# The second half of w_o in another order: one context tile between the image tiles, and the norm's first sum one tile later

## The reference: two layers of a hybrid block

```python
def rmsnorm(x, g):
    xf = x.astype(jnp.float32)
    y = xf * lax.rsqrt(jnp.mean(xf * xf, axis=-1, keepdims=True) + EPS)
    return (y * g.astype(jnp.float32)).astype(x.dtype)

def mixer_output(attn, other, pool_w, pool_scale, sconv_w, w_o):
    ...
    return jnp.concatenate([attn, pool_out, conv_out], axis=-1) @ w_o

def conv_ffn(h, w_up, w_conv, w_down):
    g, u = jnp.split(h @ w_up, 2, axis=-1)
    return (jax.nn.silu(dwconv3(g, w_conv)) * u) @ w_down

        # for each of the two layers i
        x = x + g1x * mixer_output(attn_x, rest_x, *out_w)
        x = x + g2x * conv_ffn(rmsnorm(x, norm2_g[i]) * (1 + sc2x) + sh2x, *ffn_w)

        if i < DEPTH - 1:
            attn_c = attend(qn_c, qr_c, kn_c, kr_c, v_c)
            ctx = ctx + g1c * mixer_output(attn_c, rest_c, *out_w)
            ctx = ctx + g2c * conv_ffn(rmsnorm(ctx, norm2_g[i]) * (1 + sc2c) + sh2c, *ffn_w)
```

## Time and profile before

| what | value |
|---|---|
| median of 3 runs | 1477.76 us (1477.02 to 1477.85) |
| profiled execution, its own time | 1477.17 us |
| span of its trace | 1475.4 us |
| TensorE matmuls | 1422.5 us, 96% of the span |
| VectorE | 1015.6 us, 69% |
| ScalarE | 520.1 us, 35% |
| ScalarE's split of a chunk (line 1009) | 180 of them, mean 1054 ns |
| VectorE's split of a chunk (line 1318) | 180 of them, mean 1240 ns |

### The profile page before, as it was taken

How to read it: one execution, slowest core, us unless ns; L and a number is a source line. 1 busy time by engine, 2 the same in 40 slices (tenths; PEclk the granted TensorE clock), 3 DMA queues, 4 the chain that set the end, 5 groups by cost and what they waited for, 6 DMA issues and landing times.

```text
span 1475.4 us, 20621 instructions
## 1 busy us (share of the span) xinstructions
PE 1422.5 (96%) x7932; PEld 1230.0 (83%) x7932; DVE 1015.6 (69%) x1546; ACT 520.1 (35%) x819; POOL 81.8 (6%) x139
## 2 busy tenths in 40 slices
PE   6999799999999999999999998989999999999998
PEld 4789688888888888888888888868998888888887
DVE  5588988669967566656666678788758555655555
ACT  4352765334321121212112224466535332223222
POOL 0024600000000000000000000350000000000000
PEclk9999999999999999999999999999999999999999
DMA  9732011413643343234333311301022332322324
GB/s 386 283 132 86 1 44 44 143 65 107 217 139 100 100 146 124 98 101 142 112 93 122 125 60 58 115 15 44 15 76 97 101 100 93 102 89 85 107 94 140
DMA packets 42984, 158.62 MB, mean 108 GB/s; under 512 B 5169, under 2 KB 6577, under 8 KB 41777
## 3 DMA queue, kind: packets, MB, share of 16 engines
q1 hardware_dynamic: 42928, 157.87, 31.5%
HBM read 155.76 MB, written 2.10 MB: 107 GB/s over the span
## 4 chain that ended last, share of the span: by engine, by line
PE 80%; DVE 13%; ACT 2%; DMA 2%; issue 2%; SPq 0%; DVEq 0%; ACTq 0%
PE ps L675 62%; PE ps L624 4%; PE ps L626 4%; PE ps L625 4%; DVE ada_out L1329 2%; DVE w_lo L1318 1%; DVE tmp L1407 1%; DMA ada_step<-in_w_step 1%; DVE H_lo L1416 1%; PE ps L826 1%; DVE part_sums L1569 1%; DVE ss L1396 1%; PE ps L638 1%; DMA w_raw<-in_w_main 1%; PE ps L845 1%
## 5 line engine op out<-in xcount | busy, mean ns | idle before, releaser
L675 PE MATMUL ps<-H_hi,w_hi 128*128 128x512 f32 (+1 forms) x1280 | 449.5, 351 | 6.4 <-DVE H_lo L1416 3.0
L675 PE MATMUL ps<-H_lo,w_hi 128*128 128x512 f32 (+1 forms) x1280 | 448.1, 350 | 0.0
L675 PE MATMUL ps<-H_hi,w_lo 128*128 128x512 f32 (+1 forms) x1280 | 447.7, 350 | 0.0
L1009 ACT ACTIVATE w_hi<-w_raw 128x1024 fp32r<-128x1024 f32 x180 | 187.5, 1054 | 421.6 <-PE ps L675 366.3
L675 PEld LDWEIGHTS ps<-H_hi,w_hi 128*128 128x128 f32 x1280 | 242.6, 190 | 40.7 <-issue 3.7
L675 PEld LDWEIGHTS ps<-H_hi,w_lo 128*128 128x128 f32 x1280 | 242.6, 190 | 31.7
L675 PEld LDWEIGHTS ps<-H_lo,w_hi 128*128 128x128 f32 x1280 | 242.7, 190 | 31.0
L1429 DVE SCALAR_TENSOR_TENSOR X<-ps,mod,X 128x512 f32<-128x512 f32 (+1 forms) x296 | 180.7, 644 | 113.2 <-PE ps L675 85.2
L1318 DVE TENSOR_TENSOR w_lo<-w_raw,w_hi 128x1024 fp32r<-128x1024 f32 x180 | 221.5, 1240 | 37.7 <-ACT w_hi L1009 36.7
L675 PE MATMUL ps<-inner_hi,w_hi 128*128 128x512 f32 (+1 forms) x528 | 188.1, 356 | 3.4 <-DVE w_lo L1318 1.6
L675 PE MATMUL ps<-inner_lo,w_hi 128*128 128x512 f32 (+1 forms) x528 | 187.2, 355 | 0.0
(11 more groups left out here) (195 smaller groups left out, 1854.0 us busy)
## 6 DMA issues: line engine op xcount, KB each, us to landing
w_raw<-in_w_main SPq DMA_DIRECT2D x182, 512.0 KB, 3.3
ada_raw<-in_w_ada SPq DMA_DIRECT2D x73, 512.0 KB, 4.1
ada_step<-in_w_step SPq DMA_DIRECT2D x7, 2048.0 KB, 14.8
X<-in_x SPq DMA_DIRECT2D x2, 1024.0 KB, 6.9
cb<-in_cvec SPq DMA_DIRECT2D x2, 1024.0 KB, 7.3
out_x<-X SPq DMA_DIRECT2D x8, 256.0 KB, 4.6
rtab<-in_rope SPq DMA_DIRECT2D x4, 384.0 KB, 7.2
X<-in_ctx SPq DMA_DIRECT2D x2, 512.0 KB, 7.9
```

The source lines that it names most:

```text
L675: ins = pe.matmul(job.ps(a, b), ww[:, wsl], xx[:, xk, a:b], start=first and n == 0, stop=last and n == 2)
L1009: act.activation(w_hi[c % 4][:], w_raw[c % 2][:], ACT.Copy).then_inc(chunk_hi, 1)
```

## The change

Only the order of tiles 8 to 15 changes, and what hangs on it. Tile 9 is now the context tile of row tile 4. Tiles 10 to 12 are the image tiles of row tiles 5 to 7, and 13 to 15 their context tiles. The sum over segment 0 stands ahead of tile 14 and not of tile 13. F0 is split behind tile 9 and not behind tile 12. F1 to F3 are split behind tiles 13 to 15, as before. The scaling and the making of `H_hi` and `H_lo` begin one tile later, with one piece less ahead of the end of w_o. The counts that the waits use are changed to match.

```diff
--- before.py
+++ after.py
@@ -384,6 +384,9 @@
     LAT_TURN = 6
     MIX_ORDER = [7, 6, 0, 1, 2, 5, 4, 3]
     MIX_AT = UNITS - 2
+    WO_ORDER = [(0, s, j) for s in range(2) for j in range(4)] + [(1, 0, 0), (1, 1, 0)] + [(1, 0, j) for j in (1, 2, 3)]
+    WO_ORDER += [(1, 1, j) for j in (1, 2, 3)]
+    SUM_TILE = WO_ORDER.index((1, 1, 2))
     NORM_BREAK = (1, 3, 5)
     SUM_AT = 6
     ROWS_AT, COPY_AT, TURN_AT = (0, 3, 5, 8, 11, 14), (1, 3, 5, 9, 12, 15), (2, 4, 6, 10, 13, 16)
@@ -658,7 +661,7 @@
         def norm_sum(nn, n, out):
 
             _, a, b = nsegs(nn)[n]
-            pe.wait_ge(ss_done[nn], 2 + (len(DVE_SQUARES) if nn == 0 else (KD + 4 * (nn % 2), 2 * KD)[n]))
+            pe.wait_ge(ss_done[nn], 2 + (len(DVE_SQUARES) if nn == 0 else (KD + 5 * (nn % 2), 2 * KD)[n]))
             return pe.matmul(out, ones[:], ss[:, a:b], start=nn > 0, stop=True)
 
         def norm_sum_job(nn, n):
@@ -865,14 +868,14 @@
 
             def mixed(n, ks):
 
-                i, s, j = n // 8, n // 4 % 2, n % 4
+                i, s, j = WO_ORDER[n]
                 _, a, b = nsegs(nn)[s]
                 job = Job(wo[n])
                 c = c0 + C_WO + 4 * i + j
                 if ks[0] == MIX_ORDER[0]:
                     pe.wait_ge(chunk_lo, c + 1)
                     job.open(pe)
-                    if (i, s, j) == (1, 1, 1):
+                    if n == SUM_TILE:
                         norm_sum(nn, 0, job.ps(NX, NX + nsegs(nn)[0][2])).then_inc(sum_done[nn], 1)
                 for kk in ks:
                     if n < 2 and kk >= 4:
@@ -1266,17 +1269,21 @@
             for j in range(4):
                 split_hi(c0 + C_WO + 4 + j, Job(wo[4 + j]))
                 square(nn, 4 + j, j, ya, yb, Job(wo[4 + j]))
-            for j in range(4):
-                square(nn, 8 + j, 4 + j, xa, xb, Job(wo[8 + j]))
-            root_table()
-            for j in range(4):
-                split_hi(c0 + C_FF + j, Job(wo[12 + j]))
-                if j == 0:
+            for n in range(8, 16):
+                _, sg, j = WO_ORDER[n]
+                if sg == 0:
+                    square(nn, n, 4 + j, xa, xb, Job(wo[n]))
+                    if j == 3:
+                        root_table()
+                    continue
+                split_hi(c0 + C_FF + j, Job(wo[n]))
+                if j == 1:
                     act.wait_ge(sum_done[nn], 1)
-                    root(nn, Job(wo[13]).ps(NX, NX + xb), 0).then_inc(root_done[nn], 1)
-                square(nn, 12 + j, 4 + j, ya, yb, Job(wo[12 + j]))
-                high(nn, j)
-            for n in range(4, len(pieces(nn))):
+                    root(nn, Job(wo[SUM_TILE]).ps(NX, NX + xb), 0).then_inc(root_done[nn], 1)
+                square(nn, n, 4 + j, ya, yb, Job(wo[n]))
+                if j:
+                    high(nn, j - 1)
+            for n in range(3, len(pieces(nn))):
                 high(nn, n)
                 if n == 6:
                     act.wait_ge(sum_done[nn], 2)
@@ -1715,7 +1722,7 @@
                 dve.wait_ge(cb_ok, 2)
 
             def update_part(i, s, j):
-                job = Job(wo[8 * i + 4 * s + j])
+                job = Job(wo[WO_ORDER.index((i, s, j))])
                 job.ready(dve)
                 update_x(4 * i + j, L, job, 16, seg[s:s + 1], seg[s][1])
             for j in range(4):
@@ -1729,23 +1736,25 @@
                     ada_column(ADA_A2 + 4 + j, 0, 4 * STEPS + ADA_A2 + 4 + j, 2)
                 split_lo(c0 + C_WO + 4 + j)
                 add_squares(nn, 4 + j, *seg[1][1:])
-            for j in range(4):
-                update_part(1, 0, j)
-                if L == 0 and j == 0:
-                    for s in range(2):
-                        ins = ada_bias(0, s, 4 * STEPS + ADA_A2, 5 * KD, ADA_A2 + ADA_WO)
-                    ins.then_inc(mod_done, 1)
-                if j == 1:
-                    norm_scale(nn)
-                add_squares(nn, 8 + j, *seg[0][1:])
-            for j in range(4):
-                update_part(1, 1, j)
-                scaled(nn, j)
+            for n in range(8, 16):
+                _, part, j = WO_ORDER[n]
+                update_part(1, part, j)
+                if part == 0:
+                    if L == 0 and j == 0:
+                        for s in range(2):
+                            ins = ada_bias(0, s, 4 * STEPS + ADA_A2, 5 * KD, ADA_A2 + ADA_WO)
+                        ins.then_inc(mod_done, 1)
+                    if j == 1:
+                        norm_scale(nn)
+                    add_squares(nn, n, *seg[0][1:])
+                    continue
                 if j:
-                    low(nn, j - 1)
-                add_squares(nn, 12 + j, *seg[1][1:])
+                    scaled(nn, j - 1)
+                if j > 1:
+                    low(nn, j - 2)
+                add_squares(nn, n, *seg[1][1:])
                 split_lo(c0 + C_FF + j)
-            for n in range(4, len(pieces(nn)) + 1):
+            for n in range(3, len(pieces(nn)) + 1):
                 if n < len(pieces(nn)):
                     scaled(nn, n)
                 low(nn, n - 1)
```

## The result

The changed kernel took 1482.81 us in the median of six runs (1481.83 to 1485.78), the kernel before 1477.87 us beside it (1477.02 to 1479.48). The ratio is 1.0033, 95% interval [1.0022, 1.0044]: 4.9 us slower, between 3.3 and 6.5. Forecast were +3.05 us and 1480.8 us, range 1479.0 to 1483.4. The profiled execution took 1481.83 us, its span 1480.0 us for 1475.4. Its source lines lie 3 further down on TensorE and ScalarE and 7 further down on VectorE.

What follows compares the result with a forecast made beforehand. TensorE is busy nearly all the time, and VectorE's late queue sets the end of layer 0's up projection. Layer 0's +2.15 and layer 1's +0.9 us sum to +3.05 us, median 1480.8 us, range 1479.0 to 1483.4.

Steps and rivals of the forecast that it cites:

- step (3): Layer 0, second sum: 2.58 us later, so VectorE waits 1.1 us for H_hi; layer 0 +2.15 us, bounds 1.0 and 3.9.
- (1): End of w_o: the sum over images comes one context tile, 2.88 us, later; layer 0's reciprocal moves to 318.2.
- (2): VectorE's queue behind the reciprocal: second H_lo and up projection 2.88 us late in layer 0, fifth scaling 1.01 us late.
- TensorE's reserve: Three stops near the end of layer 0's up projection, 3.04 us in all, more than TensorE's own 2.58 us delay.
- (4): Layer 1: the stop for F2 goes, a 0.85 us wait for F3's load replaces one of 0.97; end +0.9 us.
- Rival A: Clock falls in layer 1 too, or longer in layer 0: 1.7 us more, +4.75 us in all, 1482.5; chance 0.20.
- Rival B: Weights decide, not activations: layer 1 gains 1.96 us, layer 0 pays 1.01; -0.95 us, 1476.8; chance 0.20 with similar outcomes.

Runs made afterwards that it cites:

- e4: The changed kernel with ScalarE's second root in layer 0 one piece later in its queue; 1481.86 us, ratio 1.0030 to the kernel before.
- e8: The changed kernel with 20 matmuls, their result unread, filling most of the gap ahead of layer 0's up projection; 1480.68 us, ratio 1.0010 to the kernel before.
- e2: The changed kernel with the change in layer 0 only, layer 1 as before; 1481.01 us, ratio 1.0015 to the kernel before.
- e5: The changed kernel with the image sum issued inside tile 13, table load one tile earlier, root ahead of the weight split; 1481.99 us, ratio 1.0020.
- e1: The changed kernel with the old tile order, only the image sum and what hangs on it later; 1481.89 us, ratio 1.0027 to the kernel before.
- e6: The kernel before with the image sum inside tile 12, table load one tile earlier, root ahead of the split; 1477.79 us, 0.9992; repeated 1477.46 us, 0.9990.
- e3: The changed kernel with the change in layer 1 only, layer 0 as before; 1479.41 us, ratio 1.0007 to the kernel before.
- e10: The kernel before with 8 matmuls, their result unread, in the gap ahead of layer 0's up projection; 1478.34 us, ratio 0.9997.

## Why the prediction was right, by its steps

The sign, the mechanism and the range held; the centre was 2 us low (1480.8 for 1482.81), and the size of step (3) came out near by two errors that partly cancel.

(1) The sum one context tile later. Right: reciprocal forecast at 318.2, and with the 1.05 us from upstream 319.25; it stood at 319.26.

(2) The queue behind it. Right: the up projection forecast at 328.1 + 1.05 = 329.15, measured 329.12, the gap 4.96 us for 2.13 + 2.88 = 5.01; fifth scaling late by 331.80 - 329.87 - 1.05 = 0.88 for 1.01. e4 and e8, which take away what comes on top, leave 0.88 and 1.07 us of layer 0.

(3) The second sum. The mechanism was right, and its term is the one that was too small: a new wait of 1.1 us was forecast, and one of 1.39 measured. The step took over the slow phase of the kernel before. In the change the gap was longer and the clock with it lower (0.83 for 0.91 over 320 to 340 us), and the second sum came 337.99 - 334.19 - 1.05 = 2.75 us later, not 2.58. Layer 0: +2.45 for +2.15, inside its bounds of 1.0 and 3.9. With the clock that the step assumed (0.91, e2) the wait was 0.81 us and layer 0 +1.92, so for its own premise the term was too large; the longer slow phase made it too small. That TensorE's reserve would be enough held: the first stop shrank from 1.57 to 1.26 us, and the other two stayed. What the step missed is that the lower clock, cited there only as an upper bound, is a condition for the wait as a whole: at full clock there is none (e8).

(4) Layer 1. Right in kind: F2's stop went, F3's load came in its place with 0.92 us at 1113.83 for a forecast of 0.85, and TensorE stopped 0.52, 0.43, 0.56 and 1.94 us where 0.5, 0.8, 0.9 and 2 stood. The fifth scaling is late by 5.00 - 3.87 = 1.13 us for 0.9. TensorE came to its fourth step 2.1 us late for 1.75 (the second sum at 1117.78, before at 1111.82), gave 0.95 of it back at the end as forecast, and VectorE's last `H_lo` set the end.

The remaining distance is 3.59 us by the account to 4.9 by the ratio. The account lies inside the ratio's interval (from 3.3 us). One part of the distance is in the trace: 0.37 us at the start of layer 1, in code that was not changed. Another may be a longer slow phase in the other executions, for which the mean clocks and the 3.4 us by which e8 is faster speak; no trace shows such an execution, and it stays open.

Rival A came true in part. In layer 1 the clock stayed at 1.00 in the changed kernel; it fell there only in the profiled execution of e5 (0.88 over 1104 to 1118 us), and layer 1 was no longer for it (+0.84). In layer 0 the slow phase was longer, as A has it: read in windows of 1 us, full speed was missing from 325.4 to 328.8 us before and from 326.5 to 333.3 after. But 2.6 of these 6.8 us lay in the gap itself, where TensorE had nothing to do, and 4.2 us at half speed lose 2.1 us where 3.4 lost 1.7. In the profiled execution that cost 0.3 us more than forecast, not 1.7. A gap of 4.95 us went with 0.83 in e1 and with 0.91 in e2 and e4. The Trainium skill (TensorE: Matmul & The Clock Gate, the note on the warm-up in "What's actually happening") says that the number of slow matmuls varies between runs of one kernel. The two phases of the earlier trace rows lie in one execution and could not show that; two executions of one program do, e6 and its repetition, with 0.83 and 0.91 over 880 to 900 us and 1.00 and 0.83 over 180 to 200 us.

Rival B is out: the weight waits halved and nothing was won; e1, without the early split of F0, behaves the same.

## What to carry to other kernels

Where a reduction ends one stage and starts the next, the place of its matmul in the order can be worth more than the order of the tiles around it, as it was here. Count what is queued behind it on the engine that will be late (here VectorE), and look for the next thing that hangs on the same start (here the second sum and its root). Idling that another engine's queue hides may cost nothing, clock included, until a change takes the cover away: then price the gap at the lower clock.

## What the runs showed of the hardware

Ahead of the up projection of layer 0 the gaps of 2.13 us (before, e3), 4.53 us (e5) and 4.95 us (after, e1, e2, e4) went with a stretch below full clock; the gap of 1.71 us (e6, twice) and those filled with matmuls (e8, e10) did not. A mean of 0.83 is a mix of the two levels, 1.2 and 2.4 GHz: windows of 1 us show 0.50 from 327 to 333 us in the changed kernel, and 1.00 before 326 and behind 334. The low stretch began 2.6 us before the gap's end in the changed kernel, 0.4 us before it in e2, and 0.2 us behind it in the kernel before. In layer 1 stops of about 0.52, 0.43, 0.56 and 1.9 us within 6.4 us left the clock at 1.00 in the five traces that have them (after, e1, e3, e4, e8); e5, with the last three of them, had 0.88 over 1104 to 1118 us. The first 30 us of the kernel, the same code in each, had a mean clock over 20 to 30 us of 1.00 in three executions, 0.83 in seven and 0.66 in one. With other slow phases such chance moved the mark ahead of layer 0 by 0 to 3.2 us. Single profiled executions can't be compared by their spans where 1 us matters; stretches counted from a common mark can: e6 and its repetition differ by 1.9 us at the mark and by 0.02 and 0.06 us in the two layers.
